# One running order for slab loads, and modulation groups taken in pairs

## The reference, cut to what matters

```python
def _adaln(cvec, w, b):
    m = (jax.nn.silu(cvec) @ w + b)[:, None, :]     # w: 2048 x 12288, one per layer
    return jnp.split(m, 6, axis=-1)                 # shift, scale, gate, twice
def _modulate(x, g, shift, scale):
    return _rms(x, g) * (1 + scale) + shift
```

## Time and profile before

| | |
|---|---|
| timed, median of 3 | 2729.6 us (2729.39 to 2735.47) |
| profiled execution, span from first to last instruction | 2737.4 us (the page gives no other time for it) |
| PE busy | 2603.3 us, 95% |
| DVE, ACT busy | 1492.6 us (55%), 1306.1 us (48%) |
| DMA | 608.42 MB, 222 GB/s in the mean |
| granted TensorE clock, mean | 0.974 |

### The profile page before, as it was taken

One profiled execution on the slowest core, in us unless ns is written; L12 is line 12 of the kernel. 1 busy time (PEld: TensorE's weight loads), 2 busy tenths in 40 slices (PEclk: granted clock), 3 DMA queues, 4 the chain that ended last, 5 costly groups with the idle time before them and its releaser, 6 DMA issues. The chain is left out here.

```text
span 2737.4 us, 52685 instructions
## 1 busy us (share of the span) xinstructions
PE 2603.3 (95%) x20922; PEld 2366.9 (86%) x20922; DVE 1492.6 (55%) x2018; ACT 1306.1 (48%) x1819; POOL 11.9 (0%) x20
## 2 busy tenths in 40 slices
PE   6899999989999999999999999789899999999998
PEld 1488988778888888899998889788899999999997
DVE  1335445554555455466775445544765655567776
ACT  1433444364444344456555444233565555556563
POOL 0000000000000000000000000000000000000000
PEclk9999999999999999999999999699999999999999
DMA  9886555668887788864645875132455555555553
GB/s 389 335 315 235 204 210 166 250 242 303 310 305 302 290 305 295 321 247 159 220 151 166 303 293 202 51 123 93 146 186 185 187 187 184 185 188 188 185 179 108
DMA packets 170070, 608.42 MB, mean 222 GB/s; under 512 B 18688, under 2 KB 25152, under 8 KB 169648
## 3 DMA queue, kind: packets, MB, share of 16 engines
q1 hardware_dynamic: 168624, 600.33, 61.8%
q10 hardware_dynamic: 512, 2.97, 0.3%
q0 software_dynamic: 768, 2.79, 0.3%
HBM read 601.38 MB, written 4.63 MB: 221 GB/s over the span
## 5 line engine op out<-in xcount | busy, mean ns | idle before, releaser
L468 DVE TENSOR_TENSOR w_lo<-raw,w_hi 128x1024 fp32r<-128x1024 f32 x756 | 924.7, 1225 | 1022.6 <-ACT w_hi L461 1017.1
L461 ACT ACTIVATE w_hi<-raw 128x1024 fp32r<-128x1024 f32 x756 | 798.7, 1058 | 1091.3 <-PE banks L599 850.3
L597 PE MATMUL banks<-xs_ffn,w_hi 128*128 128x256 f32 x4224 | 1189.6, 282 | 5.9 <-DVE xs_ffn L753 5.6
L599 PE MATMUL banks<-xs_ffn,w_lo 128*128 128x256 f32 x4224 | 1184.1, 280 | 0.0
L598 PE MATMUL banks<-xs_ffn,w_hi 128*128 128x256 f32 x4224 | 1178.1, 279 | 0.0
L597 PEld LDWEIGHTS banks<-xs_ffn,w_hi 128*128 128x128 f32 x4224 | 795.9, 188 | 43.8 <-issue 35.4
L598 PEld LDWEIGHTS banks<-xs_ffn,w_hi 128*128 128x128 f32 x4224 | 796.0, 188 | 0.0
L599 PEld LDWEIGHTS banks<-xs_ffn,w_lo 128*128 128x128 f32 x4224 | 795.2, 188 | 0.0
L558 PE MATMUL banks<-raw,cond 128*32 128x512 f32 x1536 | 242.4, 611 | 31.2 <-DMA raw<-in_w_mod 19.3
L597 PE MATMUL banks<-xs_even,w_hi 128*128 128x256 f32 x832 | 244.6, 294 | 13.8 <-DVE xs_even L1530 7.0
L598 PE MATMUL banks<-xs_even,w_hi 128*128 128x256 f32 x832 | 235.6, 283 | 0.0
(11 more groups left out here) (305 smaller groups left out, 2107.8 us busy)
## 6 DMA issues: line engine op xcount, KB each, us to landing
raw<-in_w_mod SPq DMA_DIRECT2D x384, 512.0 KB, 6.7
raw<-in_ffn_w_up SPq DMA_DIRECT2D x352, 512.0 KB, 3.6
raw<-in_ffn_w_down SPq DMA_DIRECT2D x176, 512.0 KB, 4.2
raw<-in_even_w_in SPq DMA_DIRECT2D x72, 512.0 KB, 4.2
raw<-in_odd_w_in SPq DMA_DIRECT2D x64, 512.0 KB, 6.7
raw<-in_even_w_out SPq DMA_DIRECT2D x32, 512.0 KB, 5.1
raw<-in_odd_w_out SPq DMA_DIRECT2D x32, 512.0 KB, 3.4
raw<-in_odd_w_tail SPq DMA_DIRECT2D x8, 448.0 KB, 4.0
```

The costliest lines, as they stand in the source:

```text
L461: act.activation(w_hi[:, o % SPLIT], raw[:, s % RAW], ACT.Copy).then_inc(hi_done.sem, 1)
L468: dve.tensor_tensor(w_lo[:, o % SPLIT], raw[:, s % RAW], w_hi[:, o % SPLIT].bitcast(F32), ALU.subtract).then_inc(lo_done.sem, 1)
L597: pe.matmul(made, hi, x_hi, start=start and not second, stop=False, skip_group_check=second)
L599: return pe.matmul(made, lo, x_hi, start=False, stop=stop, skip_group_check=second)
```

## The change

**Loads.** `earlier`, `sp_first` per phase and `Phase.before` go. A new function `load_order` walks all slabs of all phases in the order of use and gives each load the place at which its slot is freed: for a slot that held a mod slab, that slab's place; for one that held own slab number n, the place of own slab n - 4, where it is split. Loads are sorted by that place and handed to the phase and iteration in which the place lies; `sp_stream` issues them there. What a load waits for is as before.

```diff
-            "mod": Phase(None, 4, 0, 0, mods=2),
-            "even_in": Phase(plain(ins["even_w_in"], 0, 9), 1, 9, KS, mods=8, one_bank=True),
...
-            ("up", 0): Phase(plain(ins["ffn_w_up0"], 0, 2), 2, 2, KS, mods=2),
-            ("up_end", 0): Phase(plain(ins["ffn_w_up0"], 4, 2), 9, 2, KS, mods=2, iter0=2),
+            "mod": Phase(None, 1, 0, 0, mods=8, two_banks=True),
+            "even_in": Phase(plain(ins["even_w_in"], 0, 9), 1, 9, KS, mods=8),
...
+            ("up", 0): Phase(plain(ins["ffn_w_up0"], 0, 2), 11, 2, KS, mods=2),
```

```diff
-            if k == 0:
-                wait(pe, mod_done.sem, f.mod_group(i, j) - (0 if f.one_bank or f.after_one_bank and j == 0 else 1))
+            p, second = j // PAIR, j % PAIR
+            if k == 0 and not second:
+                wait(pe, mod_done.sem, f.pair(i, p) - (1 if f.two_banks else 0))
+            columns = slice(2 - 2 * second, 2 - 2 * second + QUAD)
...
-                mm = pe.matmul(banks[quad:quad + QUAD, f.mod_bank(j), :], cond[:, n, :], raw[:, s % RAW, c, :],
-                               start=n < QUADS, stop=n >= KD - QUADS)
+                mm = pe.matmul(banks[quad:quad + QUAD, f.mod_bank(p), :], cond[:, n, columns], raw[:, s % RAW, c, :],
+                               start=n < QUADS and not second, stop=n >= KD - QUADS and bool(second))
```

More of the change, by code:

```diff
@@ L146, in laid_out @@
     out["gate_b"] = given["ml_gate_b"].reshape(4 * HEADS, 1)
-    out["w_mod"] = np.stack([slabs_of(w, range(0, 6 * D, SLABW)) for w in given["w_mod"]])
+    out["w_mod"] = np.concatenate([slabs_of(w, range(0, 6 * D, SLABW)) for w in given["w_mod"]])
     out["even_w_in"] = slabs_of(given["even_w_in"][0], [SLABW * g for g in EVEN_ORDER])
@@ L205, in __init__ @@
         self.slot0 = [0] * RAW
-        self.before = [("own", 0)] * RAW
+        self.loads = {}
         self.next = None
@@ L243, in plan @@
     own = group = mod = half = 0
-    held, last = [0] * RAW, [("own", 0)] * RAW
+    held = [0] * RAW
     for n, ph in enumerate(phases):
         ph.own0, ph.group0, ph.mod0, ph.half0 = own, group, mod, half
-        ph.slot0, ph.before = list(held), list(last)
+        ph.slot0 = list(held)
         assert ph.iters == 1 or ph.groups % 2 == 0
         for slot in range(RAW):
[L250 to L253, removed]
+            held[slot] += ph.loads_of(slot) * ph.iters
         own += ph.iters * len(ph.own_at)
@@ L259, in plan, with load_order @@
     assert mod == DEPTH * MOD_GROUPS
+def load_order(phases):
+    line = [(f, i, s) for f in phases for i in range(f.iters) for s in range(f.slabs)]
+    split_at, holds, due = [], [None] * RAW, []
+    for at, (f, i, s) in enumerate(line):
+        held = holds[s % RAW]
+        if held is None:
+            freed, after = -1, ("own", 0)
+        else:
+            kind, nth, where = held
+            if kind == "mod":
+                freed = where
+            else:
+                freed = split_at[nth - SPLIT] if nth >= SPLIT else split_at[0] - 1
+            after = kind, nth + 1
+        due.append((freed, at, f, i, s, after))
+        kind = f.seq[s][0]
+        if kind == "own":
+            holds[s % RAW] = "own", f.own(i, f.own_at.index(s)), at
+            split_at.append(at)
+        else:
+            holds[s % RAW] = "mod", f.mod_slab(i, f.mod_at.index(s)), at
+    due.sort(key=lambda load: load[:2])
+    first = [(f, i, s, after) for freed, at, f, i, s, after in due if freed < 0]
+    for freed, at, f, i, s, after in due:
+        if freed >= 0:
+            g, n, _ = line[freed]
+            g.loads.setdefault(n, []).append((f, i, s, after))
+    for f in phases:
+        made = [[(g is f, m - n if g is f else m, s) for g, m, s, _ in f.loads.get(n, [])] for n in range(f.iters)]
+        assert all(a == made[1] for a in made[2:-1])
+    return first
 def rolled(eng, iters, body):
@@ L429, in load_slab, with held_before, sp_first @@
             dma.then_inc(landed[slot].sem, 16)
[L431 to L435, removed]
+        def held_before(f, i, s):
+            if s >= RAW:
+                return f.used(i, s - RAW)
+            return f.used(i - 1, s + RAW * (f.loads_of(s) - 1))
+        def sp_first(sp):
+            for f, i, s, after in first_loads:
+                load_slab(sp, f, i, s, after)
         def sp_stream(sp, f):
-            def earlier(s):
-                return s - RAW + 0.5 if f.paired and f.seq[s % f.slabs][0] == "own" and s + BATCH < 2 * f.mods * MOD_SLABS else s
             def body(i, first, last):
-                for s in sorted(range(RAW, f.slabs if last else f.slabs + RAW), key=earlier):
-                    if s < f.slabs:
-                        load_slab(sp, f, i, s, f.used(i, s - RAW))
-                    else:
[L446 to L449, removed]
+                n = 0 if first else f.iters - 1 if last else 1
+                for g, m, s, after in f.loads.get(n, []):
+                    if g is f and not first and not last:
+                        load_slab(sp, f, i + (m - n), s, held_before(f, i + (m - n), s))
+                    else:
+                        load_slab(sp, g, m, s, after)
             rolled(sp, f.iters, body)
@@ L496, in split_stream, with placed @@
             return left_over(f, places)
-        def placed(f, pieces, mod_pieces):
+        def placed(f, pieces, mod_pieces, beside=()):
             return [(end + d, piece, g)
                     for ends, all_ in ((f.ends, pieces), (f.mod_ends, mod_pieces))
-                    for g, end in enumerate(ends) for d, piece in enumerate(all_) if piece is not None]
+                    for g, end in enumerate(ends) for d, piece in enumerate(all_) if piece is not None
+                    ] + [(f.slabs - MOD_SLABS, piece, 0) for piece in beside if f.mods and not f.groups]
         def run_pieces(f, places, i, s, first, left=()):
```

100 lines of the change are left out of this document (52 added, 48 removed).

## The result

| | before | changed |
|---|---|---|
| timed together, median of 5 | 2729.55 us (2725.24 to 2735.47) | 2654.53 us (2651.19 to 2675.88) |
| ratio | | 0.9735, 95% interval 0.9701 to 0.9768 |
| span of the profiled execution | 2737.4 us | 2674.1 us |

To read the numbers one thing is needed: executions of the changed kernel fall on two levels. Of 17 in three series nine lie at 2649 to 2657 us (median 2651.5) and eight at 2675 to 2683 (median 2677.6). The profiled one is of the upper level. Three executions of the kernel before, at 3208, 3208 (mean granted clock 0.74) and 7861 us, belong to a disturbed state and no reading rests on them.

What follows compares the result with a forecast made beforehand. TensorE was taken to bound the kernel, its busy time hiding loss from late loads. 20.2 + 4.4 + 20.6 + 9.0 - 2.3 = 51.9 us off the median 2729.6 gave 2678 us, range 2664 to 2706.

Steps and rivals of the forecast that it cites:

- the one on the pairs: Modulation groups taken in pairs: 20 turn blocks of 0.45 us go from TensorE, 9.0 us gained, ends 0 and 12.
- The last sentence of the prediction: A gain above 65 us would mean that TensorE's busy stretches hid more than was read.
- The load order: Loads reordered by when their buffers are freed: gains of 20.2, 4.4 and 20.6 us, less 2.3 us of cost.
- `up`: First FFN's up projection: all 21 half iterations come to 26.95 us, 20.2 us gained, ends 0 and 20.2.
- even layer: Four TensorE stalls behind late loads shrink: 8.3, 3.4, 6.7 and 2.2 us, together 20.6, ends 8 and 26.
- the fourth: Even layer's end, at 562.58: of a 4.80 us wait only 2.2 us goes, ends 0 and 4.8.
- odd projections: Layer 1's projections: five halves take 134.75 us instead of 139.16, 4.4 us gained.
- The cost at barriers: Three block ends: SyncE issues one more load after the held last split, 0.6 us each, 1.8 us lost.
- The wait that is added: With one bank, a pair's first slab waits for the previous pair's bias add: taken as 0, hidden if late slabs are cured.
- rival 3: Order does nothing and TensorE waits for the one bank, 3.1 us in each of 13 iterations: 2763 us; chance 0.04.
- Rival 1: Lateness moves on to modulation loads and attention's waits, halving the load terms: 2700 us; chance 0.15.
- Rival 2: The load order does nothing and the single bank costs nothing: 2723 us; chance 0.04.

Runs made afterwards that it cites:

- e1: The kernel before with the new order of loads alone (single groups, two banks): 2695.75 us, ratio 0.987.
- e10: The kernel before with the new load order and 160 unused bytes at the head of the even layer's and both FFNs' tiles: 2672.81 us, levels 2660 and 2688.
- e3: The changed kernel run once more, nothing altered: 2663.42 us, three of six executions on each level, the profiled one on the lower.
- e4: The kernel before run once more, nothing altered: 2729.58 us, profiled span 2730.0 us.
- e2: The changed kernel with the old order of loads (groups in pairs and one bank kept): 2703.88 us, ratio 0.9898.
- e11: The changed kernel with 32 unused bytes ahead of `xs_ffn` in both FFNs alone: 2702.24 us, ratio 0.9889.
- e14: The changed kernel with 1984 unused bytes ahead of the activations in both FFNs: 2707.82 us, ratio 0.9919.
- e17: The changed kernel with 512 unused bytes ahead of the activations in both FFNs, timed a second time: 2651.57 us, ratio 0.9737.

## Why the prediction was wrong

**The step that failed** is the one on the pairs, by a term that the sum put at nothing and gave no reason for: a change in the cost of the matmuls that stay. Its upper end of 12 us counts turn blocks and takes every other matmul at its old pitch. But the pairs shrink `mod_rows`, all later tiles move, and `xs_ffn` lands at an address where the pitch in `down` is 113.3 ns and not 116.7. With the even layer and the FFNs alone at these places (e1 to e10) that is 36 us on the lower level and about 8 on the upper (e1 2695.75, e10's upper level 2687.9), and some 5 more in layer 1's projections.

By pitches the first FFN gives 4.2 and 7.2 us (176 slabs at 1.0 ns, 88 at 3.4, 24 matmuls each), the second 28.5 or nothing. The profiles of e1 and e10 differ by 3.9 us at the first FFN's start, 11.1 in that FFN and 27.4 in the second, 42.4 in all; the medians say 36, as e1's profiled execution lies 5.3 us above its median and e10's 1.3 below.

Without the addresses the time would have been 2687 us (2695.75 - 9) to 2692 (less 3.4, what is left of 8.5), inside the range: an estimate. The low end of 2664 was itself 3 us too low by its own terms: 20.2 + 4.4 + 26 + 12 = 62.6 off 2729.6 is 2667. That changes nothing. The last sentence of the prediction named the symptom, a gain above 65 us, and was right that busy stretches hid more; what they hid was the pitch, not only lateness.

**What the pairs themselves give**: right where a row shows it. An iteration of `up` takes 53.55 us in e10 (21 halves in 562.3) against 53.09 in the changed kernel: 0.46, where 0.45 was predicted, at nearly one pitch (115.8 and 115.7 ns). That is 5.1 us for 11 of the 20 blocks. For the even layer's six no gain shows: the first FFN's own matmuls start at 549.91 us in e10 and at 549.69 in e3. The 9.0 as a whole stays unshown.

**The load order**: mechanism right, size 42.9 against 34. Each term by its own rows, e1's against those the prediction used:
- `up`: 586.15 - 566.03 = 20.1 us (20.2 predicted). Against e4's trace it is 15.5; the term came from an execution with more lateness than usual.
- even layer: the first turn block of `up` came 605.45 - 589.07 = 16.4 us earlier (20.6), the one behind the last residual 562.58 - 544.79 = 17.8. Comparing own matmul by own matmul in the two traces, the first three parts brought 8.0, 3.5 and 6.6 us (8.3, 3.4 and 6.7), so the 2 us put on without a row for the clock after the stall at 506.68 were right in size; the fourth brought 1.5 (2.2). Some 3 us are lost in other places. Half of that is the clock: behind an idle time of 2.35 us that both kernels have, e1's fell to half and a w_mod batch at 435.11 took 3.56 us. First e1, then before:

```profile
434.00:440.00 6.00, 6.00 (x39) 2.98 (x38) 2.11 (x4) 2.09 (x7) 0.00 (x0) 0.72 0.46 137
```

```profile
441.00:447.00 6.00, 6.00 (x53) 4.44 (x52) 2.20 (x4) 2.09 (x7) 0.00 (x0) 1.00 0.59 184
```

- odd projections: five halves take 1626.10 - 1488.51 = 137.59 instead of 139.16, 1.6 us (4.4). Three of the five are now 26.95, as in `up`; the last two stay long, 28.81 and 27.92 (before 28.93 and 27.62), with no batch above 2.3 us in them. The prediction took all length above 26.95 for lateness, and in these two it wasn't.

**The cost at barriers** (1.8 for three): right. TensorE's first matmul behind each in the changed kernel, then in the one before:

```profile
1383.62 0.98 PE L731 MATMUL banks<-const,sums 128*128 128x2 f32 x4 [6.52 <-PEq L887]
...
1649.35 0.85 PE L1698 MATMUL banks<-const,prj 128*128 128x128 f32 x6 [3.68 <-PEq L887]
...
1903.47 0.77 PE L731 MATMUL banks<-const,sums 128*128 128x2 f32 x3 [6.06 <-PEq L887]
```

```profile
1438.46 0.77 PE L692 MATMUL banks<-const,sums 128*128 128x2 f32 x3 [5.46 <-PEq L848]
...
1709.57 0.66 PE L1662 MATMUL banks<-const,prj 128*128 128x128 f32 x2 [3.16 <-PEq L848]
...
1967.29 0.98 PE L692 MATMUL banks<-const,sums 128*128 128x2 f32 x4 [5.46 <-PEq L848]
```

1.06 + 0.52 + 0.60 = 2.2 us more. That the one issue more is the cause wasn't tried by itself.

**The wait that is added**: right, hidden with the new order and, as e2 shows, only with it. e2 lies 19 us above what addresses and pairs alone would give (2729.5 - 36 - 8.5 = 2685). At the addresses of before it would be at some 2740 to 2745, slower by 10 to 15 us, an estimate that no run tests: rival 3 had its place and sign, and two to three times the size (2763). The prediction gives a rule on banks as what makes this wait necessary. The kernel needs it in any case, since the next pair's first matmuls overwrite the bank that VectorE still has to read; no run leaves the wait out. **Rival 1**: its sign, batches of 3 us and more, stands at three places ahead of the steady part of `up` (3.34, 3.80 and 3.15 us against 1.92, 4.5 us in all), and nowhere in `up` from 611.69 on. **Rival 2**: refuted by e1.

## What to carry to other kernels

When a change resizes a tile, list which others move, and compare the count of matmuls in a stretch that the change does not touch: busy share and granted clock say nothing there. A kernel that is bound by a stream of matmuls should be timed with a few unused bytes ahead of its moving operand before any edit is credited with a few per cent, and more than five executions are needed where a time has two levels. A queue that is served in order should hold its loads in the order in which their buffers come free; a long half that repeats in the same place of a loop is the sign that it doesn't.

## What the runs showed of the hardware

- The pitch of fp32r matmuls of 128x256 went from 113.3 to 120.0 ns with the address of the moving operand, at a granted clock of 1.0 throughout. 32 bytes were enough for 5 ns; steps of 512 and 1024 bytes changed nothing. By which rule it goes stays open: of the places tried, 64 bytes below to 64 bytes above the changed kernel's, its own is the best, and whether the distance to `w_hi`, which never moved, or the place itself counts wasn't tried.
- The Trainium skill, TensorE: Matmul & The Clock Gate, Back-to-back issue gap, gives N / 2.4 + 2.5 ns for an isolated gap at full clock, and by that an estimate of 109.2 ns for 256 columns. The matmuls here are a stream with a weight load before each, and the stages come no nearer than 113.3 ns.
- At one and the same address the second FFN has 113.3 or 117.8 ns for its whole length, drawn anew with each execution, while the first FFN has 113.3 in `down` every time it was profiled. Only one execution of a run is profiled, so the other executions' levels are read from their times; in the nine profiles at this address with the new order or with 160 bytes the level of the time and the pitch agree. What draws the level is open. It is not drawn once for a whole execution: at unmoved addresses `uq` has 118.3 to 118.6 ns in e11 and e14 and 113.4 to 113.8 in the other kernels with pairs and `uq`'s tiles at the same places, and `out_b` of layer 1 has 117.8 in e2, e11, e14 and e17 and 113.3 in the others, while e2's second FFN is at 113.3. Nor are the levels shown to be equally likely: e2 was on one level in six executions of six.
